# Two transformer blocks on one core: who squares for the norms, tiles read before weights are split, loop entries, and the order inside a recurrence

## The chip, the cores and the metric

One NeuronCore of a Trainium2 chip runs the whole program; everything else of the chip is idle. The metric is the device time of one execution in microseconds, taken as the median of several runs.

## The reference, cut to what matters

Two blocks in a row, 256 tokens of width 1024, all in float32. The first block has two layers and carries 256 context tokens along until its second layer; the second block has one layer with a gated recurrence and one with a pooling mixer.

```python
# first block, for each of 2 layers (512 tokens in layer 0; in layer 1 the context ends after the mixer's keys)
m = mixer(x * (1 + sc1) + sh1)         # Fourier mix, neighbourhood attention, latent attention, gated merge, @ w_out
x = layer_norm(ALPHA * x + (1 + g1) * m, ln1_g, ln1_b)
f = (silu(h @ w_gate) * (h @ w_up)) @ w_down          # h = x * (1 + sc2) + sh2, hidden width 2816
x = layer_norm(ALPHA * x + (1 + g2) * f, ln2_g, ln2_b)

# second block, layer 0 mixes by the recurrence, layer 1 by pooling
h = modulate(rms_norm(x, norm_mix_g), sh_m, sc_m)
gate = gelu(h @ w_y + b_y)
xr = causal_conv4(h @ w_in + b_in)
r, i = sigmoid(blockdiag(xr, w_a) + b_a), sigmoid(blockdiag(xr, w_x) + b_x)    # 4 blocks of 256 x 256 each
log_a = 8 * r * log_sigmoid(lam);  a = exp(log_a)
s = scan(a, sqrt(-expm1(2 * log_a)) * (i * xr))       # s_t = a_t * s_(t-1) + u_t along the tokens
y = (s * gate) @ w_out + b_out                        # layer 1: pool_mixer(h) * pool_scale
x = x + gt_m * y
x = x + gt_f * (square(relu(modulate(rms_norm(x, norm_ffn_g), sh_f, sc_f) @ w1)) @ w2)   # hidden width 4096
out = rms_norm(x, final_norm_g)
```

## The kernel before, in words

The residual stream stays in SBUF as `X`, eight tiles of 128 features by up to 512 tokens, and every product is built from two-part operands: a weight is `SH + SL`, an input `AH + AL` (or `HH + HL` for the hidden layer, `YH + YL` for branches and the convolved input), and each step takes three matmuls: high by high, high by low, low by high (L473, L474, L475).

The work is a hand-written list `seq` of sections. Most are a `Unit`: four output tiles, one PSUM bank each (banks 0 to 3), each over `kt` steps (8 mostly). Its weights come in two transfers of 1 MB (`RAW[0]`, `RAW[1]`, issued on SyncE, L425), each of which may start when the second split of the pair's old content is done. ScalarE copies a quarter of the weights to `SH` (`split_act`, L431), VectorE subtracts to get `SL` (`split_dve`, L437). There is one `SH` and one `SL` per tile position, so a unit's successor is split while the unit computes: as soon as the products of tile `m` are finished, ScalarE and VectorE split the successor's tile `m`, and then read tile `m` of their own unit out of its bank. A unit marked `by_k` does all four tiles' steps k by k (so that it can start while a norm still makes its inputs) and is finished with all four at once; one marked `late` leaves the last k-steps of its first two tiles to the end of those two.

What a unit does with a tile is in `read_act` and `read_dve`: `Residual` adds it to `X` on VectorE (L678), and behind it GpSimd keeps sums over features for the next norm (`stats_pool`, L646 to L657): per tile a total `S1`, a square `SQ` (L655) and the sum of squares `S2` (L657). `Norm` then sums over partitions with matmuls against ones into banks 4 and 5 (L808 to L814: `S1`, `S2`, the last tile of `X`, and its square `NT`, which ScalarE made at L885), makes mean and variance on VectorE (L829 to L839), the root on ScalarE (L889), the reciprocal on VectorE (L845), and then tile by tile centres, scales, casts to `AH` (L875) and subtracts to `AL` (L877). The norm of layer-norm kind that ends the first block is followed by a second, rms one.

Some units carry a side job: a 2 MB piece of the modulation weights `SIDE`, multiplied by the conditioning vectors on TensorE (L353), turned (L317) into banks 4 and 5 and added into `MODT` on VectorE (L375, `side.dve`).

Pairs of like units in the MLPs run in hardware loops of two turns. `write_programs` enters a loop (L2080) after TensorE has waited for the reader of every bank that the loop will use. There are four such entries where TensorE has to wait: the MLPs of both layers of both blocks.

The recurrence in order: a norm; two `Conv` units (`w_in`; per tile a bias copy to `XR` on ScalarE, L1636, the first tap on VectorE, L1646, three more, L1650, then `YH`, `YL`, L1653 and L1655); the first half of `w_y` (`Gelu`); four `GateBlocks` units of two k-steps (`w_a`, `w_x`, weights of 128x256 per split; sigmoid, L1677); `Lru` (tanh L1569, exp L1573, square L1577, sqrt L1580 on ScalarE, in two halves of four tiles; L1592, L1597 and the scan L1599 on VectorE); the second `Gelu`; `LruOut` (product with the gate on GpSimd, L1616, copy to `AH` on ScalarE, L1623, `AL` on VectorE, L1628); and `w_out`, two `Residual` units that add a bias first (L672, L675).

`PoolMix` multiplies by the pooling matrices `MIX` and `BT`, which `LoadWindows` brings from HBM after the first MLP of the second block (L1002), reads each of its tiles in two steps, and leaves the squares to GpSimd (L1754).

```python
        def act(self, e, K):                                    # Unit
            for m in range(4):
                e.wait_ge(sem["products"], K.at("products", self.freed(m)))
                if self.nxt:
                    self.nxt.split_act(e, K, m, 1 if self.loaded else 2)
                self.read_act(e, K, m)
```

## Time and profile before

| what | value |
|---|---|
| median of 3 runs | 2353.78 us |
| lowest and highest of them | 2350.56 and 2356.4 us |
| the profiled execution's own time | 2332.89 us |
| its span in the trace | 2331.1 us |
| mean granted TensorE clock in it | 0.947 of full |
| TensorE matmul busy | 2040.3 us |
| VectorE, ScalarE, GpSimd busy | 1216.7, 821.3, 192.4 us |

The rows come from one profiled execution, whose time is 20.9 us under the median of the other runs. Times in them are microseconds from the start of the span unless they say ns. `L473` is line 473 of the kernel. PE is TensorE's matmul side, PEld its weight loads, DVE is VectorE, ACT ScalarE, POOL GpSimd. In a timeline row the bracket at the end gives how long the engine had been idle before it and whose result ended that idle time. "PEclk" is the clock that TensorE was granted, as a share of 2.4 GHz.

### The profile page before, as it was taken

How to read it: one execution, taken by the hardware profiler on the slowest of the kernel's cores; microseconds unless marked ns; L12 is line 12 of the kernel's file. 1: busy time of each engine (PE TensorE's matmuls, PEld its weight loads, DVE VectorE, ACT ScalarE, POOL GpSimd, SP SyncE). 2: the span in 40 equal slices, each digit the busy share in tenths (PEclk: the TensorE clock that was granted, in tenths of full speed). 3: DMA queues.
4: the chain of work that ended last, by engine and by line, in shares of the span. 5: the costliest groups of instructions: out<-in, count | busy, mean ns of one | idle time of the engine just before them, and what ended most of it. 6: DMA issues, size and time to landing. Idle time of an engine off the chain costs nothing.

```text
span 2331.1 us, 31990 instructions
## 1 busy us (share of the span) xinstructions
PE 2040.3 (88%) x12456; PEld 1641.9 (70%) x12456; DVE 1216.7 (52%) x2075; ACT 821.3 (35%) x1314; POOL 192.4 (8%) x186
## 2 busy tenths in 40 slices
PE   3999899789979999998897979799968579986997
PEld 1777557247757777775774836689967579985997
DVE  6323544563564334345435564565666676666665
ACT  3422342262241121213424334343444633433343
POOL 0000000000300004012000000200330320011001
PEclk8999899899989999998999989899989789998999
DMA  7416025004534545545470704755532345642553
GB/s 271 146 60 218 30 73 167 0 2 162 170 129 156 195 145 192 169 155 169 138 250 1 239 1 159 258 180 168 193 109 73 115 138 164 191 152 91 175 186 109
DMA packets 280855, 332.07 MB, mean 142 GB/s; under 512 B 13286, under 2 KB 229788, under 8 KB 280604
## 3 DMA queue, kind: packets, MB, share of 16 engines
q1 hardware_dynamic: 268704, 323.05, 42.4%
q10 hardware_dynamic: 12028, 7.32, 1.2%
q8 instruction: 84, 1.38, 0.2%
q14 instruction: 39, 0.32, 0.0%
HBM read 329.31 MB, written 1.05 MB: 142 GB/s over the span
## 4 chain that ended last, share of the span: by engine, by line
PE 67%; issue 11%; DVE 9%; ACT 5%; DMA 5%; POOL 2%; ACTq 0%; POOLq 0%; DVEq 0%; SPq 0%
PE ps L473 17%; PE ps L474 16%; PE ps L475 16%; PE ps L1144 3%; DVE SL L437 3%; PE ps L353 3%; ACT SH L431 2%; PE ps L1166 2%; PE ps L1152 1%; DMA RAW<-in_w_in 1%; PE ps L1315 1%; DVE RSTD L845 1%; PE ps L1321 1%; DMA RAW<-in_ffn_w 1%; POOL S L657 1%
## 5 line engine op out<-in xcount | busy, mean ns | idle before, releaser
L437 DVE TENSOR_TENSOR SL<-RAW,SH 128x1024 fp32r<-128x1024 f32 (+3 forms) x460 | 529.2, 1154 | 836.0 <-ACT SH L431 834.7
L431 ACT ACTIVATE SH<-RAW 128x1024 fp32r<-128x1024 f32 (+3 forms) x460 | 447.6, 980 | 1110.2 <-PE ps L475 917.9
L473 PE MATMUL ps<-AH,SH 128*128 128x256 f32 (+1 forms) x2048 | 676.7, 330 | 84.8 <-DVE AL L877 28.5
L474 PE MATMUL ps<-AL,SH 128*128 128x256 f32 (+1 forms) x2048 | 668.1, 326 | 0.0
L475 PE MATMUL ps<-AH,SL 128*128 128x256 f32 (+1 forms) x2048 | 666.9, 326 | 0.0
L473 PEld LDWEIGHTS ps<-AH,SH 128*128 128x128 f32 x2048 | 401.3, 196 | 151.3 <-issue 53.3
L475 PEld LDWEIGHTS ps<-AH,SL 128*128 128x128 f32 x2048 | 400.9, 196 | 29.3
L474 PEld LDWEIGHTS ps<-AL,SH 128*128 128x128 f32 x2048 | 401.6, 196 | 27.4
L473 PE MATMUL ps<-HH,SH 128*128 128x256 f32 (+1 forms) x992 | 307.3, 310 | 8.8 <-DVE HL L747 4.5
L474 PE MATMUL ps<-HL,SH 128*128 128x256 f32 (+1 forms) x992 | 304.0, 306 | 0.0
L475 PE MATMUL ps<-HH,SL 128*128 128x256 f32 (+1 forms) x992 | 304.0, 306 | 0.0
L473 PEld LDWEIGHTS ps<-HH,SH 128*128 128x128 f32 x992 | 187.5, 189 | 29.7 <-issue 8.6
L475 PEld LDWEIGHTS ps<-HH,SL 128*128 128x128 f32 x992 | 187.1, 189 | 10.9
L474 PEld LDWEIGHTS ps<-HL,SH 128*128 128x128 f32 x992 | 187.1, 189 | 10.2
L649 POOL TENSOR_TENSOR S<-X 128x256 f32<-128x256 f32 (+1 forms) x9 | 13.1, 1451 | 1932.5 <-DVE X L678 1914.5
L353 PE MATMUL ps<-SIDE,CC 128*32 128x512 f32 x704 | 90.4, 634 | 14.6 <-DVE VAR L836 7.8
L473 PE MATMUL ps<-YH,SH 128*128 128x256 f32 (+1 forms) x224 | 75.7, 338 | 8.3 <-DVE YL L1071 3.0
L1200 ACT ACTIVATE PR<-ps,SM 128x512 f32<-128x512 f32 (+1 forms) x96 | 59.2, 616 | 65.8 <-PE ps L1152 52.6
L474 PE MATMUL ps<-YL,SH 128*128 128x256 f32 (+1 forms) x224 | 73.5, 328 | 0.0
L475 PE MATMUL ps<-YH,SL 128*128 128x256 f32 (+1 forms) x224 | 73.5, 328 | 0.0
L1240 DVE TENSOR_REDUCE SM<-ps 128x1 f32<-128x512 f32 (+1 forms) x96 | 57.4, 598 | 8.4 <-PE ps L1144 7.1
L1152 PEld LDWEIGHTS ps<-CON,PR 128*128 128x128 f32 x320 | 37.9, 147 | 31.5 <-issue 16.8
(240 smaller groups left out, 2032.9 us busy)
## 6 DMA issues: line engine op xcount, KB each, us to landing
SIDE<-in_w_mod SPq DMA_DIRECT2D x45, 2048.0 KB, 8.1
...
```

Of the source, the lines that this page charges most:

```text
L353: ins = e.matmul(PS[4][32 * g:32 * g + 32, :], CC[:, k, :], SIDE[:, k, :], start=k < 4, stop=k >= 4)
L431: e.activation(SH[:, m, 0:kt, :], RAW[p][:, 0:kt, o:o + P], ACT.Copy).then_inc(K.up("weight_high"), 1)
L437: e.tensor_tensor(SL[:, m, 0:kt, :], RAW[p][:, 0:kt, o:o + P], SH[:, m, 0:kt, :].bitcast(F32), ALU.subtract).then_inc(K.up("weight_low"), 1)
L473: e.matmul(ps, SH[:, m, k, :], xh, start=k == 0, stop=False)
L474: e.matmul(ps, SH[:, m, k, :], xl, start=False, stop=False)
L475: ins = e.matmul(ps, SL[:, m, k, :], xh, start=False, stop=k == self.kt - 1)
L657: e.tensor_tensor(S2[:, c0:c1], S2[:, c0:c1], SQ[:, c0:c1], ALU.add).then_inc(K.up("pool_done"), 1)
L1144: e.matmul(self.scores_of(n), q, k, start=True, stop=True).then_inc(K.up("scores_done"), 1)
L1152: ins = e.transpose(PS[self.TURNED[n % 2]][:, j * P:(j + 1) * P], PR[:, n % 2, j * P:(j + 1) * P], IDENT)
L1166: ins = e.matmul(o[64 * i:64 * i + 64, 0:256], V[:, c0 // P + j, 64 * (h + i):64 * (h + i) + 64], PTS[pair % 2][:, i, j, :], start=j == 0, ...
L1200: e.activation(PR[:, n % 2, 0:c1 - c0], self.scores_of(n), ACT.Exp, bias=SM[:, n % 4:n % 4 + 1], accum_out=SM[:, 4 + n % 4:5 + n % 4]).the ...
L1240: e.tensor_reduce(SM[:, n % 4:n % 4 + 1], ps, AX.X, ALU.max, negate=True).then_inc(K.up("max_done"), 1)
```

## The change

- **Tile first, weights second.** In every unit, ScalarE and VectorE read the finished tile out of its bank and only then split the successor's weights. VectorE also adds the side job (`side.dve`) before its last split.
- **Squares of the norms on ScalarE.** `Residual.read_act` squares the tile before the one just finished, into a ring of two buffers `SQR`; GpSimd only adds totals and squares. The norm's sums go to banks 6 and 7, which the side job does not use. In `PoolMix` ScalarE squares tiles in pairs, 512 wide, and the norm behind it sums both halves and the last pair with four matmuls.
- **Loop entries.** TensorE does not wait for a bank's reader in front of a loop where the loop's own first wait is on the same reader.
- **The recurrence.** The first tap of the convolution goes to ScalarE. The four `GateBlocks` units become one unit `Gates` with two transfers and four splits of 128x1024 over all eight banks. ScalarE does eight sigmoids, eight tanh, eight sigmoids, eight exp, eight sqrt and then the gelus, with the splits of the next units between them; the squares of the decay go to VectorE, 128x1024 at a time, and the scans run in two groups of four. `LruOut` is split in two and writes `Y8H`, `Y8L` with VectorE alone. The output bias is added into `X` by GpSimd ahead of time (`LruBias`), and the first `w_out` unit takes its inputs with four late k-steps in place of `by_k`.
- **The pooling matrices** get a place of their own and are loaded in front of the second block.

The diff, cut to its core:

```diff
+    MIX, BT = (MACC[:, 4 * j:4 * j + 4, :].rearrange("p g (t n) -> p g t n", t=2) for j in range(2))
...
@@ class Unit @@
         def act(self, e, K):
             for m in range(4):
                 e.wait_ge(sem["products"], K.at("products", self.freed(m)))
+                self.read_act(e, K, m)
                 if self.nxt:
                     self.nxt.split_act(e, K, m, 1 if self.loaded else 2)
-                self.read_act(e, K, m)
...
         def dve(self, e, K):
...
-                if self.nxt:
-                    self.nxt.split_dve(e, K, m)
                 e.wait_ge(sem["products"], K.at("products", m + 1))
                 self.read_dve(e, K, m)
                 if m == 3 and self.side:
                     self.side.dve(e, K, 0)
+                if self.nxt:
+                    self.nxt.split_dve(e, K, m)
...
+    class GeluLru(Gelu):
+        def act(self, e, K):
+            for k in range(KT):
+                e.activation(LA[:, k, :], LA[:, k, :], ACT.Exp, scale=DER[:, 6, k:k + 1]) \
+                    .then_inc(K.up("decay_done"), 1)
+            self.split_next(e, K, (0, 1))
+            for k in range(KT):
+                e.wait_ge(sem["one_minus_a2"], K.at("one_minus_a2", 4 * (k // 4) + 4))
+                e.activation(LT[:, k, :], LT[:, k, :], ACT.Sqrt).then_inc(K.up("root_done"), 1)
+            self.split_next(e, K, (2, 3))
+            for m in range(4):
+                self.read_act(e, K, m)
...
+        def dve(self, e, K):
+            for half in range(2):
+                t = slice(4 * half, 4 * half + 4)
+                e.wait_ge(sem["decay_done"], K.at("decay_done", 4 * half + 4))
+                e.tensor_tensor(XR[:, t, 0:SEQ], LA[:, t, :], LA[:, t, :], ALU.mult).then_inc(K.up("dve_done"), 1)
...
+            for m in (0, 1):
+                self.nxt.split_dve(e, K, m)
+            self.scan(e, K, 0)
+            for m in (2, 3):
+                self.nxt.split_dve(e, K, m)
+            self.scan(e, K, 1)
...
+    def stats_pool(e, K, first, tokens, mean):
...
+        def add_square(t):
+            e.wait_ge(sem["tile_squared"], K.at("tile_squared", t + 1 if first else t - 2))
+            if t > 1:
+                e.wait_ge(sem["square_added"], K.own("square_added"))
+            e.tensor_tensor(S2[:, c0:c1], S2[:, c0:c1], SQR[:, t % 2, c0:c1], ALU.add).then_inc(K.up("square_added"), 1)
...
     class Residual(Columns):
+        def read_act(self, e, K, m):
+            t = self.tile0 + m - 1
+            if not self.stats or t < 0:
+                return
+            c0, c1 = self.tokens
+            e.wait_ge(sem["dve_read"], K.at("dve_read", m))
...
+            to = S2[:, c0:c1] if t == 0 else SQR[:, t % 2, c0:c1]
+            e.activation(to, X[:, t, c0:c1], ACT.Square).then_inc(K.up("tile_squared"), 1)
...
@@ class Norm @@
-            for b in (4, 5):
+            for b in (6, 7):
                 reader, count = K.bank[b]
                 e.wait_ge(sem[reader], K.value(reader, count))
...
+            if self.paired:
+                e.matmul(PS[7][:, 0:n], ONES[:, :], S2[:, n:2 * n], start=False, stop=False)
+                e.wait_ge(sem["tile_squared"], K.at("tile_squared"))
+                e.matmul(PS[7][:, 0:n], ONES[:, :], SQR[:, 1, 0:n], start=False, stop=False)
+                ins = e.matmul(PS[7][:, 0:n], ONES[:, :], SQR[:, 1, n:2 * n], start=False, stop=True)
...
     class LoadWindows(Load):
         def act(self, e, K):
-            e.wait_ge(sem["dve_read"], K.at("dve_read"))
-            e.wait_ge(sem["products"], K.at("products"))
             e.wait_ge(sem["hidden_low"], K.at("hidden_low"))
...
+    class LruOut:
...
         def dve(self, e, K):
+            e.wait_ge(sem["products"], K.at("products", -self.products))
+            for j, k in enumerate(self.tiles):
+                e.wait_ge(sem["gated_done"], K.at("gated_done", j + 1))
+                e.tensor_copy(Y8H[:, k, :], XC[:, k, :]).then_inc(K.up("dve_done"), 1)
+                e.wait_ge(sem["dve_done"], K.own("dve_done"))
+                e.tensor_tensor(Y8L[:, k, :], XC[:, k, :], Y8H[:, k, :].bitcast(F32), ALU.subtract) \
...
+    class LruBias:
...
+            e.tensor_tensor(DER[:, 8, :], vec("lru_b_out_2", 0, 8), mod(2, 2, 2), ALU.mult).then_inc(K.up("pool_done"), 1)
+            e.wait_ge(sem["pool_done"], K.own("pool_done"))
             for k in range(KT):
+                e.tensor_scalar(X[:, k, 0:SEQ], X[:, k, 0:SEQ], DER[:, 8, k:k + 1], None, ALU.add) \
...
     class Conv(Copied):
         def read_act(self, e, K, m):
...
+            e.activation(XC[:, i, :], XR[:, i, 0:SEQ], ACT.Identity, bias=vec("lru_conv_b_2", i),
+                         scale=vec("lru_conv_w_2", i)).then_inc(K.up("tap_done"), 1)
...
-            e.tensor_scalar(xc, XR[:, i, 0:SEQ], vec("lru_conv_w_2", i), vec("lru_conv_b_2", i), ALU.mult, ALU.add) \
...
+    class Gates(Columns):
...
+        def act(self, e, K):
+            for p in range(2):
+                for i in range(KT):
+                    e.wait_ge(sem["products"], K.at("products", KT * p + i + 1))
+                    e.activation((GI if p else LA)[:, i, :], PS[i][:, 0:SEQ], ACT.Sigmoid,
+                                 bias=vec("lru_b_x_2" if p else "lru_b_a_2", i)).then_inc(K.up("act_read"), 1)
+                for m in range(2):
+                    self.nxt.split_act(e, K, 2 * p + m, 2)
+                if p == 0:
...
+                    for k in range(KT):
+                        e.activation(LT[:, k, :], LA[:, k, :], ACT.Tanh, scale=DER[:, 7, k:k + 1]) \
+                            .then_inc(K.up("act_done"), 1)
...
     class PoolMix(Residual):
+        def read_act(self, e, K, m):
+            to = S2[:, :] if m == 0 else SQR[:, m % 2, :]
+            e.wait_ge(sem["dve_read"], K.at("dve_read", m + 1))
...
+            e.activation(to.rearrange("p (j n) -> p j n", j=2), X[:, 2 * m:2 * m + 2, 0:SEQ], ACT.Square) \
...
+    seq.append(LoadWindows())
     seq.append(rms("norm_mix_g_2", 0, 2, 0, summed=True))
...
-    seq.append(gelu[0])
-    seq += [GateBlocks(w=A["lru_w_a_2"][0], u=u, dst=LA, bias="lru_b_a_2") for u in range(2)]
-    seq += [GateBlocks(w=A["lru_w_x_2"][0], u=u, dst=GI, bias="lru_b_x_2") for u in range(2)]
-    seq += [Lru(), gelu[1], LruOut()]
...
+    gelu[1].bank0 = 4
+    seq += [LruBias(), conv[0], conv[1], Gates(), gelu[0], LruOut(0, 4), gelu[1], LruOut(1, 8)]
...
-                     first=half == 0, mean=False, bias="lru_b_out_2", ready=("input_low", True), by_k=half == 0,
+                     first=half == 0, mean=False, folded=half == 0, rhs=(Y8H, Y8L), ready=("hidden_low", True),
+                     late=0 if half else 4, scale=lambda s, i: mod(2, 2, 2, i)) for half in range(2)]
...
-    seq.append(LoadWindows())
...
+    seq.append(rms("norm_ffn_g_2", 8, 3, 3, paired=True))
...
@@ write_programs @@
-                            eng.wait_ge(sems[before], count)
+                            if before != reader or v - stride[reader] < count:
+                                eng.wait_ge(sems[before], count)
```

TensorE at the third loop entry, where the first MLP of the second block passes from its first unit into the loop (`AH` is the norm's output, `HH` the hidden layer of the unit before). Before:

```order
L475 MATMUL ps<-HH,SL 128x256
L2080 UNCONDITIONAL_BRANCH [waits dve_read]
L2080 ISA
L466 REGISTER_ALU [waits weight_low]
L473 MATMUL ps<-AH,SH 128x256 [waits input_low,dve_read]
```

and with the change:

```order
L475 MATMUL ps<-HH,SL 128x256
L2152 UNCONDITIONAL_BRANCH
L2152 ISA
L466 REGISTER_ALU [waits weight_low]
L473 MATMUL ps<-AH,SH 128x256 [waits input_low,dve_read]
```

The wait at the branch is gone, and the one at the first matmul, which is counted per bank, stays.

ScalarE in the recurrence (`LA` the decay, `LT` what becomes the factor of the input, `GI` the input gate, `SH<-RAW` a split), before, from the first tanh on:

```order
L1569 ACTIVATE LT<-LA,DER 128x256 x4
L1573 ACT_TABLE_LOAD
L1573 ACTIVATE LA<-LA,DER 128x256 x4
L1577 ACTIVATE XR<-LA 128x256 x4
L1580 ACT_TABLE_LOAD
L1580 ACTIVATE LT<-LT 128x256 x4
L1569 ACT_TABLE_LOAD
L1569 ACTIVATE LT<-LA,DER 128x256 x4
L1573 ACTIVATE LA<-LA,DER 128x256 x4
L1577 ACTIVATE XR<-LA 128x256 x4
L1580 ACT_TABLE_LOAD
L1580 ACTIVATE LT<-LT 128x256 x4
```

and with the change, from the first sigmoid on:

```order
L1734 ACTIVATE LA<-ps,VEC 128x256 x8
L431 ACTIVATE SH<-RAW_54 128x1024 x2
L1742 ACTIVATE LT<-LA,DER 128x256 x8
L1734 ACTIVATE GI<-ps,VEC 128x256 x8
L431 ACTIVATE SH<-RAW_55 128x1024 x2
L593 ACT_TABLE_LOAD
L593 ACTIVATE LA<-LA,DER 128x256 x8
L431 ACTIVATE SH<-RAW_54 128x1024 x2
L598 ACT_TABLE_LOAD
L598 ACTIVATE LT<-LT 128x256 x8
L431 ACTIVATE SH<-RAW_55 128x1024 x2
```

The two rounds of tanh, exp and sqrt have become one, tanh has moved in front of the second eight sigmoids, and eight splits of 128x1024 stand between the steps.

ScalarE at the end of the recurrence's `w_out`, before:

```order
L431 ACTIVATE SH<-RAW_54 128x1024 x2
L431 ACTIVATE SH<-RAW_55 128x1024 x2
L885 ACTIVATE NT<-X 128x256
L887 ACT_TABLE_LOAD
L887 ACTIVATE SM<-ONES 128x1
```

and with the change:

```order
L761 ACTIVATE SQR<-X 128x256
L431 ACTIVATE SH<-RAW_54 128x1024
L761 ACTIVATE SQR<-X 128x256
L431 ACTIVATE SH<-RAW_54 128x1024
L761 ACTIVATE SQR<-X 128x256
L431 ACTIVATE SH<-RAW_55 128x1024
L761 ACTIVATE SQR<-X 128x256
L431 ACTIVATE SH<-RAW_55 128x1024
L958 ACTIVATE NT<-X 128x256
L960 ACT_TABLE_LOAD
L960 ACTIVATE SM<-ONES 128x1
```

A square of 128x256 now stands ahead of each split.

## Rows read from the trace of the kernel before

**Rows 1.** The page: busy time of each engine, and shares of the chain that ended last.
```profile
PE 2040.3 (88%) x12456; PEld 1641.9 (70%) x12456; DVE 1216.7 (52%) x2075; ACT 821.3 (35%) x1314; POOL 192.4 (8%) x186
...
PE 67%; issue 11%; DVE 9%; ACT 5%; DMA 5%; POOL 2%; ACTq 0%; POOLq 0%; DVEq 0%; SPq 0%
```

**Rows 2.** Windows: length; PE, PEld, DVE, ACT, POOL busy (count); PEclk, DMA share, GB/s.
```profile
777.00:790.00 13.00, 9.87 (x33) 7.97 (x34) 2.69 (x5) 1.86 (x3) 0.00 (x0) 0.74 0.68 225
1578.00:1582.00 4.00, 3.91 (x18) 3.94 (x19) 0.00 (x0) 0.00 (x0) 0.00 (x0) 0.50 1.04 339
1610.00:1630.00 20.00, 20.00 (x170) 20.00 (x170) 12.40 (x19) 7.90 (x10) 0.00 (x0) 1.00 0.52 175
1723.10:1727.00 3.90, 3.78 (x8) 2.50 (x8) 0.04 (x1) 0.00 (x0) 0.00 (x0) 0.50 0.04 13
1940.00:1953.00 13.00, 11.50 (x83) 11.53 (x84) 5.54 (x11) 3.77 (x6) 0.00 (x0) 0.87 0.31 90
```

**Rows 3.** Waits of TensorE: us in total, times, longest us.
```profile
PEld ps L473 <- DVE X L678: 14.8, 4, 4.1
PE ps L1144 <- DVE MODT L375: 13.2, 2, 6.6
```

**Rows 4.** Groups of instructions: count, busy us, mean ns, idle before and its releasers.
```profile
L437 DVE TENSOR_TENSOR SL<-RAW,SH 128x1024 fp32r<-128x1024 f32 x376 | 470.6, 1255 | 626.7 <-ACT SH L431 626.2
L431 ACT ACTIVATE SH<-RAW 128x1024 fp32r<-128x1024 f32 x376 | 394.8, 1058 | 866.4 <-PE ps L475 742.0 <-DMA RAW<-in_w_in 35.3 <-DMA RAW<-in_w_ffn_gate 29.0
L657 POOL TENSOR_TENSOR S<-S,SQ 128x256 f32<-128x256 f32 x36 | 34.0, 943 | 2.8
L678 DVE SCALAR_TENSOR_TENSOR X<-ps,DER,X 128x256 f32<-128x256 f32 x96 | 43.0, 475 | 0.0
L1650 DVE SCALAR_TENSOR_TENSOR XC<-XR,VEC,XC 128x256 f32<-128x256 f32 x24 | 11.6, 485 | 0.9
L1677 ACT ACTIVATE LA<-ps,VEC 128x256 f32<-128x256 f32 x8 | 3.7, 466 | 0.0
```

**Rows 5.** Timeline: the sums of the norm that ends the first block.
```profile
1723.14 1.22 PE L808 MATMUL ps<-S,ONES 128*128 128x256 f32 x2 [6.61 <-POOL S L657]
...
1726.96 0.42 DVE L829 TENSOR_SCALAR MU<-ps 128x256 f32<-128x256 f32 x1 [7.39 <-PE ps L814]
```

**Rows 6.** Timeline: where TensorE starts again at five other norms.
```profile
647.21 1.10 PE L808 MATMUL ps<-S,ONES 128*128 128x512 f32 x2 [3.18 <-DVE MODT L375]
...
1502.39 1.22 PE L808 MATMUL ps<-S,ONES 128*128 128x256 f32 x2 [4.64 <-POOL S L657]
...
1878.67 1.22 PE L809 MATMUL ps<-S,ONES 128*128 128x256 f32 x2 [5.98 <-POOL S L657]
...
2089.32 0.55 PE L1704 MATMUL ps<-SH,AH 128*128 128x256 f32 x1 [7.44 <-DMA MIX<-in_constants]
...
2115.27 1.22 PE L809 MATMUL ps<-S,ONES 128*128 128x256 f32 x2 [13.40 <-POOL S L1754]
```

**Rows 7.** Window of the recurrence, first split to last product of w_out; columns as rows 2.
```profile
1758.40:1872.70 114.30, 79.75 (x585) 75.95 (x583) 77.15 (x131) 63.20 (x118) 28.93 (x25) 0.90 0.35 111
```

**Rows 8.** Timeline inside the recurrence: last conv tile, ScalarE's steps, start of w_out.
```profile
1789.77 0.43 DVE L1655 TENSOR_TENSOR YL<-XC,YH 128x256 fp32r<-128x256 f32 x1
...
1816.74 1.71 ACT L1569 ACTIVATE LT<-LA,DER 128x256 f32<-128x256 f32 x4
...
1818.46 1.28 ACT L1573 ACT_TABLE_LOAD   x1
1819.76 1.71 ACT L1573 ACTIVATE LA<-LA,DER 128x256 f32<-128x256 f32 x4
...
1844.44 0.55 PE L473 MATMUL ps<-AH,SH 128*128 128x256 f32 x1 [16.65 <-DVE AL L1628]
```

**Rows 9.** The page: the products of the hidden layer, and what they wait for.
```profile
L473 PE MATMUL ps<-HH,SH 128*128 128x256 f32 (+1 forms) x992 | 307.3, 310 | 8.8 <-DVE HL L747 4.5
```

**Rows 10.** Timeline: where TensorE enters the Fourier mix.
```profile
110.06 2.18 PE L1031 MATMUL ps<-DFT,FT 128*128 128x256 f32 x9 [1.65 <-DVE MODT L375]
```

266 lines of the change are left out of this document (130 added, 136 removed).

## The prediction

> **What bounds the kernel now.** I read the page first. TensorE is busy with matmuls for 88% of the span and holds 67% of the chain that ended last; the next owner is "issue" with 11%, then VectorE with 9% [rows 1]. So the kernel is a stream of matmuls with holes, and an edit is worth what it takes out of the holes, plus what the clock does after them. Then the windows: in a steady stretch TensorE runs 170 matmuls in 20 us at granted clock 1.00, the level of 2.4 GHz, while after a hole it runs 18 in 4 us at 0.50, the level of 1.2 GHz, where the steady stretch would have run 34 [rows 2]. A hole thus costs its own length and a stretch at half speed behind it. Then the waits, for the holes with a name in the change: four at the loop entries, 14.8 us, and two in front of the neighbourhood attention, 13.2 us [rows 3]. The groups give durations [rows 4], and the timeline shows the holes at the norms [rows 5, 6] and in the recurrence [rows 7, 8].
>
> **Loop entries.** TensorE waits in front of the loop for a VectorE read that is queued behind the split of the last weights, 14.8 us over four entries [rows 3]. With the wait gone, the first matmul waits for its own bank only, which was read three tiles earlier; I leave 0.4 for each branch: 14.8 - 1.6 = 13.2 saved. The clock was 0.74 in the 13 us around one entry (of the two in the first block) and 0.87 around one of the second [rows 2]; if two entries are of each kind, the share lost is 13 x (0.26 + 0.26 + 0.13 + 0.13) = 10.1. I take 9, with 0 and 10.1 as ends. Sum 22.2.
>
> **Norm ends.** Before, GpSimd makes total, square and sum of squares for each tile, and TensorE has idled 6.61 us when the last sum comes [rows 5]. Afterwards ScalarE's square of tile 6 (0.45 us, the length of a 256-wide read [rows 4]) starts when the last product ends, and GpSimd's addition (0.94 [rows 4]) follows: TensorE starts at about 1.4. The last square comes after one split of 1.06 [rows 4], at about 2.0, behind the first matmuls. That is 5.2 saved; the eight sum matmuls behind took 3.78 us at clock 0.50 [rows 2], and after a short hole part of that comes back, 0.8. In all:
> - end of the first block: 5.2 + 0.8 = 6.0
> - first norm of layer 1: 4.64 [rows 6] less 1.4, and 1.2 from the clock: 4.4
> - norm behind the recurrence: 5.98 [rows 6] less 1.4, and 0.5: 5.1
> - the two norms over 512 tokens: TensorE waits 3.18 there for the side job's addition [rows 6]. With other banks that wait is not needed, but squares of 512 (0.63) and an addition of 1.3 (both estimates, twice the elements of the rows for 256, less the fixed part) bring about 2.0: 1.2 each, 2.4
> - norm behind PoolMix: 13.40 us of hole [rows 6], of which GpSimd's seven squares are the end. Afterwards VectorE and ScalarE take turns tile by tile: a read in two steps 0.9, a square of 512 0.63, a split 1.06, a split 1.25 [rows 4]: 3.8 us for each of four tiles, so the wait falls by 3.1
> - norm before PoolMix 0.5; the final norm loses 0.8, since ScalarE's square stands between VectorE's last read and the addition.
>
> Together 2.4 + 4.4 + 6.0 + 5.1 + 3.1 + 0.5 - 0.8 = 20.7.
>
> **Pooling matrices.** TensorE waited 7.44 us for them [rows 6]. Loaded far ahead, the wait ends with the norm's second `AL` at 5.8: 1.6 saved.
>
> **Recurrence.** Before, 114.3 us pass from the first split behind the first `Conv` to the last product of `w_out`, with TensorE busy for 79.75 [rows 7]. The new order, laid out with the old durations from 1758.4 on:
> - VectorE per conv tile: three taps of 0.485 [rows 4], cast and subtract 0.7, split 1.25 [rows 4]: 3.4, where it was 3.8. But the second `Conv`'s first weights wait for the whole first tile: 2.2 later. Eight tiles end at 1785.5 to 1787; before, the last `YL` was at 1789.8 [rows 8].
> - ScalarE then is the chain: eight sigmoids 3.7 [rows 4], two splits 2.1, eight tanh 3.4 (four were 1.71 [rows 8]), eight sigmoids 3.7, two splits 2.1, a table load 1.3 [rows 8], eight exp 3.4, two splits 2.1, a table load 1.3, eight sqrt 2.7, two splits 2.1, a table load 1.3, four gelus 1.9: 31.1 us from 1787, to about 1815 to 1818. Two table loads are gone, 2.6 us.
> - VectorE behind it: eight scans with splits between, the second half of `w_y` on TensorE, and the last `Y8L` at about 1830 to 1831. Before, `w_out` started at 1844.44 after 16.65 us of hole [rows 8]. The first k-steps of `w_out` start earlier, its last 16 + 32 + 32 steps of three matmuls at 0.12 us follow: end at about 1850.9.
> So the stretch falls from 114.3 to 92.5: **21.7** saved. I bound this from both sides by 5 (ScalarE's chain with every split waiting for a late transfer) and 30 (all of the hole of 16.65 [rows 8] gone, and three quarters of the other 17.9 in which TensorE stands, 114.3 - 79.75 - 16.65).
>
> What a table load costs is seen in the trace: it takes 1.28 us, starts 10 ns after the last tanh ended, and the exp starts 20 ns behind it [rows 8]. The Trainium skill, "ScalarE: Activation LUTs", section "What ACT_TABLE_LOAD costs", gives about 1.28 us for the load and about 1.38 for a drain beside it. By that, two loads fewer would be worth 5.3 us rather than 2.6, and my stretch would be 2.7 shorter; the trace agrees with the first part and shows no second one.
>
> **Small places.** Side additions come one split earlier at VectorE: the Fourier mix waits 0.35 rather than 1.65 [rows 10], twice, 2.6; the attention's two waits [rows 3] shorten by 1.0 each, 2.0. The hidden layer's low half is ready a split earlier, so its waits of 4.5 [rows 9] go, with 0.6 of bank waits: 5.1. Against this, splits come later by a read in all units: a `by_k` unit whose four tiles end together gives its successor its first weights 0.4 to 1.2 us later, 3.4 in sum, and the values 1.2. Net 2.6 + 2.0 + 5.1 - 3.4 - 1.2 = 5.1. The delayed split costs nothing elsewhere, because the units' weights are split a whole unit ahead; its cover is the idle time of VectorE, 52% busy [rows 1]. If the cover is gone, a unit waits for `SL`, which is the last rival.
>
> **Sum.** 22.2 + 20.7 + 1.6 + 21.7 + 5.1 = 71.3. The rows are of an execution of 2332.9 us, which comes to 2261.6; that execution is 20.9 under the median of the runs, and I subtract the same from the median: 2353.8 - 71.3 = **2283**.
>
> **Rivals.**
> - *Half of the norm and recurrence gains, 15%.* ScalarE becomes the bound where it has splits, squares and table loads in one queue. For: in the recurrence it is busy 63 of 114 us already [rows 7]. Against: the norms' square is 0.45 beside 1.06. It loses (20.7 + 21.7)/2 = 21: 2304.
> - *The clock falls in new places, 8%.* The side job's rows run early, holes move, and the clock term of 9 fails with as much again lost at other stretches like those of 1.2 GHz [rows 2]: 2300.
> - *The clock term is nothing, 5%.* If what the rows call a granted clock did not slow the matmuls, shorter holes would give back their length only: 9 less, 2292. Against it: 18 matmuls in 4 us at 0.50, 170 in 20 at 1.00 [rows 2]. The Trainium skill, "TensorE: Matmul & The Clock Gate", section "Seeing it yourself", warns that clock events in a trace have been seen to be unreliable; by that this term could be 0. The trace disagrees, since the spacing of the matmuls changes with the clock shown.
> - *The loop entry does nothing, 2%.* The matmul behind the branch waits for the same read, so the change does not do what it says there: 22 less, 2305.
> - *Slower, 4%.* Reading first makes each split later by a read (0.47 for a 256-wide one on ScalarE, 0.475 on VectorE [rows 4], 1.1 for a gated or squared one). The buffer `RAW` comes free later by both, its transfer lands later, and in the 256-token stages (36 units in layer 1, 42 in the second block), where a unit lasts some 11.6 us (96 matmuls of 0.12) and needs 2 MB, TensorE waits for `SL` at each unit. This cancels everything from 71.3/78 = 0.9 us per unit on. At 1.2 us it costs 94: 2376. Against it: in the steady stretch DMA is at 0.52 and TensorE never idle [rows 2], so there is slack of several us per unit.
>
> **Numbers.** The forecast has 66%, the rivals the rest. Predicted 2283. Its own ends: recurrence +17 / -8, clock +9 / -1, small places and norms some 8 either way. With the first two rivals inside, the range is 2266 to 2312, which leaves out about 2 in 10. A measurement of this kernel can tell about 0.3%, some 7 us, from no change. Faster by more than that: all cases but the last, and a rest of 1%: 0.95; slower 0.04; same 0.01.
>
> **What would show it.** In the profile after: no wait of the first products at the four loop entries for L678's successor, and a clock of 1.00 in the 13 us behind; TensorE's hole in front of the norm's sums at 1.5 to 2 rather than 4.6 to 6.6; no wait for the pooling matrices; 27 table loads on ScalarE in place of 30; and the recurrence at 92 us in place of 114. The prediction is wrong if the splits' waits of TensorE ("PEld L473 <- DVE SL") grow by tens of us in the stages of 256 tokens, if a hole of over 4 us stands at the loop entries with another releaser, or if the recurrence's stretch stays over 105.

## The result, and the profile after

The changed kernel takes 2253.3 us (median of 4 runs, 2250.97 to 2256.18) where the kernel before takes 2353.7: a ratio of 0.9574, with a 95% interval of 0.9557 to 0.9592. That is 100 us less, where 71 were forecast, and it lies below the range, whose low end was 2266. The direction was right and the size was not.

Between the two profiled executions, the sum that was forecast, the spans differ by 81.9 us (2331.1 to 2249.2). The other 18.5 us are in how quick the two profiled executions were: the one before lay 20.8 us under its median, the one of the changed kernel 2.3 under its own. The first experiment below explains it.

Part 1 of the page of the changed kernel:

```profile
PE 2021.5 (90%) x12460; PEld 1630.8 (73%) x12460; DVE 1221.5 (54%) x2045; ACT 842.7 (37%) x1357; POOL 139.3 (6%) x121
```

Span less PE's busy time is the time in which TensorE stands: 290.8 before [rows 1], 227.7 now, 63.1 less. The matmuls themselves, of about the same number, take 18.8 less. So the gain has two kinds, holes and clock, and they are kept apart below.

The windows of the changed kernel, with the columns of [rows 2]: two loop entries in the first block (TensorE enters the loops at 777.4 and 1551.8), one in the second (1873.1), a steady stretch, and the sums of the norm that ends the first block.

```profile
776.00:789.00 13.00, 13.00 (x64) 10.40 (x63) 4.05 (x7) 2.72 (x3) 0.00 (x0) 1.00 0.97 322
1546.00:1559.00 13.00, 13.00 (x114) 13.00 (x114) 7.66 (x10) 5.06 (x6) 0.00 (x0) 1.00 0.79 248
1872.00:1885.00 13.00, 13.00 (x112) 13.00 (x112) 8.71 (x15) 5.85 (x8) 0.00 (x0) 1.00 0.60 184
1576.00:1596.00 20.00, 20.00 (x169) 20.00 (x169) 11.85 (x17) 8.50 (x11) 0.00 (x0) 1.00 0.63 206
1691.00:1693.10 2.10, 1.99 (x8) 1.44 (x8) 1.38 (x4) 1.95 (x4) 0.01 (x1) 1.00 0.35 123
```

The clock at the entries is 1.00 where it was 0.74 and 0.87 [rows 2], and the eight sum matmuls take 1.99 us where they took 3.78. The waits at the entries, 14.8 us over four [rows 3], are gone. In the waits of the changed kernel below, the first line is the wait of weight loads for split weights, which the prediction's slower rival had growing by tens of us; it was 56.0 before. The second is the wait in front of the two neighbourhood attentions, 13.2 before. The third has the engine and releaser of the old waits at the entries, but stands elsewhere: four waits of 0.8 us of the weight loads inside the down products of the first block's layer 0 (at 896, 921, 1043 and 1068 us), for which the matmuls do not stop.

```profile
PEld ps L473 <- DVE SL L437: 28.8, 18, 6.6
...
PE ps L1215 <- DVE MODT L374: 11.1, 2, 5.5
...
PEld ps L473 <- DVE X L732: 3.4, 4, 0.8
```

The timeline of the changed kernel at the norms of [rows 5, 6] (in this order: first norm of layer 1, end of the first block, behind the recurrence, pooling product, behind PoolMix):

```profile
1485.28 0.70 PE L876 MATMUL ps<-S,ONES 128*128 128x256 f32 x2 [0.39 <-POOL S L711]
...
1691.07 0.70 PE L876 MATMUL ps<-S,ONES 128*128 128x256 f32 x2 [1.46 <-POOL S L711]
...
1817.85 0.70 PE L877 MATMUL ps<-S,ONES 128*128 128x256 f32 x2 [1.31 <-POOL S L711]
...
2017.92 0.55 PE L1774 MATMUL ps<-SH,AH 128*128 128x256 f32 x1 [5.80 <-DVE AL L950]
...
2039.29 1.22 PE L877 MATMUL ps<-S,ONES 128*128 128x256 f32 x2 [7.58 <-POOL S L1828]
```

The holes of 4.64, 6.61 and 5.98 are 0.39, 1.46 and 1.31, and TensorE starts on the pooling matrices after 5.80 us, which is the wait for the norm, all as forecast; the one behind PoolMix fell by 5.8 rather than 3.1.

The window of the recurrence, first read behind the first `Conv` to the last product of `w_out`, and a table load in it:

```profile
1724.50:1816.60 92.10, 76.10 (x586) 74.66 (x584) 73.10 (x105) 60.09 (x102) 21.23 (x21) 0.93 0.45 143
```
```profile
1770.00 1.28 ACT L598 ACT_TABLE_LOAD   x1
1771.29 0.42 ACT L598 ACTIVATE LT<-LT 128x256 f32<-128x256 f32 x1
```

92.1 us, where 92.5 were laid out and 114.3 stood before [rows 7].

### The profile page after: what moved, and what is told of

It reads as the page before. It is cut to its first block and busy times, and to the rows that moved or that the text cites. A ratio compares the mean times of both kernels' runs of the same rounds, so it can differ in the third digit from the quotient of the medians.

```text
span 2249.2 us, 31789 instructions
## 1 busy us (share of the span) xinstructions
PE 2021.5 (90%) x12460; PEld 1630.8 (73%) x12460; DVE 1221.5 (54%) x2045; ACT 842.7 (37%) x1357; POOL 139.3 (6%) x121
## 3 DMA queue, kind: packets, MB, share of 16 engines
q8 instruction: 84, 1.38, 0.3%
## 5 line engine op out<-in xcount | busy, mean ns | idle before, releaser
L437 DVE TENSOR_TENSOR SL<-RAW,SH 128x1024 fp32r<-128x1024 f32 (+2 forms) x448 | 525.2, 1176 | 482.8 <-ACT SH L431 477.1
L473 PE MATMUL ps<-AH,SH 128*128 128x256 f32 (+1 forms) x1984 | 652.9, 329 | 57.7 <-DVE AL L950 39.4
L474 PE MATMUL ps<-AL,SH 128*128 128x256 f32 (+1 forms) x1984 | 645.7, 325 | 0.0
L475 PE MATMUL ps<-AH,SL 128*128 128x256 f32 (+1 forms) x1984 | 644.6, 325 | 0.0
L431 ACT ACTIVATE SH<-RAW 128x1024 fp32r<-128x1024 f32 (+2 forms) x448 | 443.4, 997 | 457.3 <-PE ps L475 309.4
L473 PEld LDWEIGHTS ps<-AH,SH 128*128 128x128 f32 x1984 | 384.5, 194 | 119.3 <-issue 65.8
L475 PEld LDWEIGHTS ps<-AH,SL 128*128 128x128 f32 x1984 | 384.3, 194 | 29.2
L474 PEld LDWEIGHTS ps<-AL,SH 128*128 128x128 f32 x1984 | 384.6, 194 | 27.4
L473 PE MATMUL ps<-HH,SH 128*128 128x256 f32 (+1 forms) x992 | 305.3, 308 | 2.7 <-DVE HL L691 1.6
L473 PEld LDWEIGHTS ps<-HH,SH 128*128 128x128 f32 x992 | 186.3, 188 | 22.4 <-issue 4.2
L475 PEld LDWEIGHTS ps<-HH,SL 128*128 128x128 f32 x992 | 186.4, 188 | 10.9
L705 POOL TENSOR_TENSOR S<-X 128x512 f32<-128x512 f32 (+1 forms) x6 | 10.9, 1816 | 1524.2 <-DVE X L732 1524.2
L732 DVE SCALAR_TENSOR_TENSOR X<-ps,DER,X 128x256 f32<-128x256 f32 x96 | 43.2, 478 | 94.0 <-PE ps L475 94.0
L473 PE MATMUL ps<-YH,SH 128*128 128x256 f32 (+1 forms) x256 | 85.1, 332 | 9.5 <-DVE SL L437 6.4
L711 POOL TENSOR_TENSOR S<-S,SQR 128x256 f32<-128x256 f32 (+1 forms) x54 | 50.9, 942 | 472.3 <-ACT SQR L761 472.3
```

The lines of the kernel that those rows point to most:

```text
L431: e.activation(SH[:, m, 0:kt, :], RAW[p][:, 0:kt, o:o + P], ACT.Copy).then_inc(K.up("weight_high"), 1)
L437: e.tensor_tensor(SL[:, m, 0:kt, :], RAW[p][:, 0:kt, o:o + P], SH[:, m, 0:kt, :].bitcast(F32), ALU.subtract).then_inc(K.up("weight_low"), 1)
L473: e.matmul(ps, SH[:, m, k, :], xh, start=k == 0, stop=False)
L474: e.matmul(ps, SH[:, m, k, :], xl, start=False, stop=False)
L475: ins = e.matmul(ps, SL[:, m, k, :], xh, start=False, stop=k == self.kt - 1)
L705: e.tensor_tensor(S1[:, c0:c1], so_far, X[:, t, c0:c1], ALU.add).then_inc(K.up("pool_done"), 1)
```

## The experiments

Times are medians of 5 to 12 runs beside runs of the kernel before on the same chip; its medians there were 2348.3, 2348.9, 2347.7 and 2351.7. "us saved" is against that median. The 95% intervals of their ratios come to 6 to 8 us either way. "Hole time" is the span of the profiled execution less the time in which TensorE's matmuls are busy.

### The kernel before, again

No edit. Expected:

> The kernel before, unchanged, with a profile taken on this chip. What is to be told: its profiled execution was 2332.9 us while its runs have a median of 2353.7; the change saved 81.9 us between the two spans and 100.4 between the medians. Theory A (the trace of before was an unusually quick execution; the missing 18.6 us sit at places that have nothing to do with the change): the new profiled execution takes 2350 to 2356, and the 20 us lie in stretches like the first block's attention. Theory B (profiling itself makes this kernel quicker, by its timing at the loop entries or at the clock): the new one is again at 2330 to 2336 while the runs stay at 2353.

Measured: 2351.1, from 2346.5 to 2361.6; 19 other runs of it on this chip lay between 2334.1 and 2357.8. Its new profiled execution has a span of 2352.7. Part 1 of its page, and windows of the two neighbourhood attentions, first in it, then in the execution shown ahead of the prediction:

```profile
PE 2061.7 (88%) x12456; PEld 1654.3 (70%) x12456; DVE 1217.8 (52%) x2075; ACT 821.5 (35%) x1314; POOL 192.3 (8%) x186
```
```profile
266.00:354.00 88.00, 80.64 (x368) 47.58 (x364) 45.35 (x124) 39.83 (x111) 0.00 (x0) 0.86 0.15 49
1256.00:1314.00 58.00, 52.87 (x272) 31.66 (x272) 30.53 (x72) 24.95 (x60) 0.00 (x0) 0.78 0.17 56
```
```profile
265.00:347.00 82.00, 74.63 (x366) 44.31 (x363) 45.35 (x124) 39.61 (x111) 0.00 (x0) 0.93 0.16 52
1245.00:1296.00 51.00, 45.28 (x272) 27.84 (x268) 30.32 (x72) 24.78 (x59) 0.00 (x0) 0.92 0.19 63
```

TensorE stands for 291.0 us in one and 290.8 in the other: the same. All of the 21.6 us between them is matmul time at a lower granted clock, and 11.6 of it lies in these two stretches (5.5 and 6.1 between the first matmuls of each attention and of what follows it; the windows are rounded to whole us). Theory A holds, though only about half of the difference lies in the attentions. Over the 31 runs of this batch the time broadly follows the mean granted clock: 0.946 goes with 2334 us, 0.933 with 2357. The profile ahead of the prediction, at 0.947, was one of the quickest executions that this kernel has.

### The loop entries alone, and undone

```diff
-                            eng.wait_ge(sems[before], count)
+                            if before != reader or v - stride[reader] < count:
+                                eng.wait_ge(sems[before], count)
```

Expected, for this edit on the kernel before:

> The kernel before with the loop-entry edit alone. By the forecast it saves 22.2 us (13.2 of waits, 9 of clock): about 2331. Rival (clock term is nothing): 13 us, 2340. Rival (the wait only moves): 0 to 2 us.

Measured: 2326.1 (ratio 0.990, 0.987 to 0.994), 22.2 us saved, as forecast; the interval is 14 to 31 us. In its profile all four waits at the entries are gone, and the hole time is 280.9 us, 10.1 less than in the repeated kernel before, where 13.2 were forecast. The rest of the 22 is matmul time.

The same lines put back in the changed kernel. Expected:

> The changed kernel with the old wait at the loop entries. If the parts add up, it loses the same 22 us: about 2275. If tiles read first already let the last read come sooner, the wait is shorter by one split of 1.25 us at each of four entries, and it loses 12 to 18: 2266 to 2271.

Measured: 2259.1, 5.8 more than the 2253.3 of the changed kernel, and 8.5 more than its second median below. It is less than either expectation. Its waits have `PEld ps L473 <- DVE X L732: 10.9, 8, 2.4`: four of these eight are at the entries, 7.6 us with the longest 2.4, where the kernel before has 14.8 and 4.1; the other four are the 0.8 us ones that the changed kernel has too. The entries are worth 22 us alone and 6 to 8 beside the rest.

### The order of reading and splitting, undone and alone

In the changed kernel:

```diff
                 e.wait_ge(sem["products"], K.at("products", self.freed(m)))
-                self.read_act(e, K, m)
                 if self.nxt:
                     self.nxt.split_act(e, K, m, 1 if self.loaded else 2)
+                self.read_act(e, K, m)
...
+                if self.nxt:
+                    self.nxt.split_dve(e, K, m)
                 e.wait_ge(sem["products"], K.at("products", m + 1))
                 self.read_dve(e, K, m)
                 if m == 3 and self.side:
                     self.side.dve(e, K, 0)
-                if self.nxt:
-                    self.nxt.split_dve(e, K, m)
```

Expected:

> The changed kernel with the weights split first and the tiles read second, in every unit that keeps the common order. By the forecast the order brings 9.7 us in small places and costs 4.6, and behind it stand parts of the norm terms, since the square would wait for a split of 1.06 us: loses 5 to 15, 2258 to 2268. Rival (reading first is what delays splits and transfers): it gains, 2240 to 2250. If the unexplained 18.6 us belong to this part, it loses 25 or more.

Measured: 2291.6, 38 to 41 us more than the changed kernel, and 21 to 23 us more hole time (249.1). The expected 5 to 15 was too little.

The same order put into the kernel before, alone. Expected:

> The kernel before with tiles read first and weights split second, and nothing else. Undone in the changed kernel this order was worth 38 us. If the order alone brings that, by the loop entries (the last read is no longer queued behind a split), by the units that need all four banks, and by the norms' sums, it takes 2308 to 2318. If it needs the squares on ScalarE to bring it, 2330 to 2340. If it steadies the clock in the neighbourhood attention (0.86 and 0.74 in the repeated execution of before, 0.88 and 0.93 in the changed kernel), its runs lie within 6 us of each other.

Measured: 2288.2 (ratio 0.975, 0.972 to 0.978), from 2283.4 to 2294.6: 60.7 us saved by this one edit, over half of the whole, and 20 us beyond the quickest that was expected. The clock in the attentions is not steadied by it, since later runs fall on either side. The page of this run:

```profile
PE 2022.1 (88%) x12456; PEld 1632.7 (71%) x12456; DVE 1246.8 (55%) x2075; ACT 823.7 (36%) x1314; POOL 209.9 (9%) x186
```

Against the repeated kernel before, TensorE stands 27 us less (291.0 to 264.0 of a span of 2286.1) and its matmuls take 39.6 less; some 15 of these are the two attentions, which came out quick in this execution. Of the 27, 6 are at the loop entries (14.9 us of waits in the repeated kernel before, 8.7 here) and about 10 in front of the norms' sums, places that the forecast had given to other edits. The wait of weight loads for split weights is 54.8 us here and 58.0 there, so the later split delayed nothing. How a shorter hole gives back more than itself is seen at one loop entry of the first block, here 17 us around it in the repeated kernel before and in this run:

```profile
784.00:801.00 17.00, 13.27 (x56) 10.55 (x55) 3.32 (x5) 2.60 (x3) 0.00 (x0) 0.80 0.59 200
```
```profile
769.00:786.00 17.00, 15.49 (x76) 12.52 (x75) 4.63 (x6) 4.15 (x5) 0.00 (x0) 1.00 0.61 208
```

The wait of TensorE in it (put down to the side job's addition) fell from 3.73 to 1.50 us, and the granted clock behind it is 1.00 instead of 0.80: 76 matmuls in 17 us instead of 56. In this stage (the norm of layer 0 to the next one) the hole time fell by 3.0 us and the length by 10.7:

```profile
653.90:1087.40 433.50, 418.13 (x2000) 311.00 (x2001) 179.30 (x266) 100.05 (x120) 46.94 (x38) 0.97 0.49 163
```
```profile
643.30:1066.10 422.80, 410.38 (x2000) 307.54 (x2001) 188.99 (x263) 100.10 (x120) 56.27 (x38) 0.99 0.49 167
```

### The order on one engine at a time

The changed kernel with the first half of the edit above (ScalarE splits first), and with the second (VectorE; `PoolMix` keeps the changed order there). Expected:

> The changed kernel with ScalarE splitting first and reading second, VectorE as changed. Of the 38 us of the order, ScalarE's part is the tiles that ScalarE reads (gates, silu, squared relu) and the norm squares, each of which would wait for a split of 1.06 us. If the order matters on the way of a tile to the next unit's input, both engines' parts count and this one loses 10 to 20 (2262 to 2272). If it is VectorE alone (reads of the residual, side additions), it loses under 5.

Measured: 2269.8, 19 more than the changed kernel (2250.6).

> The changed kernel with VectorE splitting first and reading second (in PoolMix it stays as changed), ScalarE as changed. VectorE's split is 1.25 us and first waits for ScalarE's, which now comes after ScalarE's read: a read on VectorE is late by up to 2.3 us. If the bank and the loop entries wait for VectorE's read, this is the larger half: loses 20 to 40 (2272 to 2292). If under 10, the order's worth lies on ScalarE.

Measured: 2293.8, 43 more: as much as both halves together, and a little over the 20 to 40 expected. The hole time is 236.8 and 250.7 in these two, against 226.5 to 227.7 in the changed kernel. So VectorE's order carries it; ScalarE's 19 vanish when VectorE already splits first. The reason given for the 43 is argued from the waits, not isolated: VectorE's reads end the waits at entries, at the side additions and at units that need all four banks. In this run the two attentions wait 13.3 us for `MODT` and four norms up to 6.1 us for GpSimd, against 11.1 and at most 2.0.

### Both edits on the kernel before

> The kernel before with tiles read first and with the loop-entry edit. Alone they saved 60.7 and 22.2 us. If they remove different waits they add up: 2266. If the wait at the entries was mostly the read queued behind the split, reading first has already taken it, and the pair is worth what the entry edit was in the changed kernel, 5.8, more than the order alone: 2280 to 2284.

Measured: 2281.7 (0.969 to 0.974 of before), 66.1 us saved, against 60.7 for the order alone; 60.7 and 22.2 would be 82.9. The two edits meet at the entries: the read that TensorE awaited there was queued behind the split, and the order alone takes 6 of the 15 us of waits. Yet it is not the hole time that fails to add up. It is 252.4 here, 38.6 less than in the repeated kernel before, and 27.0 and 10.1 for the two alone make 37.1; why the 6 us are not missing was not traced. What does not add up is the clock behind the holes. In the 13 us around the entries (3 before TensorE goes on, 10 after) it was 0.74, 0.74, 0.74 and 0.87 in the repeated kernel before, and the order alone had brought three of the four to 1.00, so the second edit had little left to give back. The second entry in these two, first in the repeated kernel before, then with the order alone:

```profile
1593.50:1606.50 13.00, 10.00 (x62) 10.03 (x63) 4.06 (x6) 2.88 (x5) 0.00 (x0) 0.74 0.51 163
```
```profile
1547.60:1560.60 13.00, 10.87 (x91) 10.71 (x91) 6.79 (x10) 5.71 (x7) 0.00 (x0) 1.00 0.52 164
```

### Squares back on GpSimd

A first form put the squares on GpSimd but kept the new division of tiles between units, with tile 3 in the second one. Expected:

> The changed kernel with the squares of the layer norms and of the MLP norms back on GpSimd (PoolMix keeps its pairs). By the forecast's norm terms it loses what GpSimd's chain costs at five norms, 2.4 + 4.4 + 6.0 + 5.1 + 0.5 less the part that the other banks give: 10 to 18, so 2263 to 2271. Rival: GpSimd starts earlier than before because tiles are read a split sooner, so the square's place is worth only 5 to 8: 2258 to 2261.

Measured: 2316.0, 65 more. That was the edit and not the part: tile 3's square waited for the last read of the second unit, since it counted reads from that unit's start, and the waits of TensorE show GpSimd's chain behind it at `PEld ps L874 <- POOL S L714: 48.5, 4, 15.1`. The second form takes `stats_pool` of the kernel before:

```diff
-                stats_pool(e, K, self.first, self.tokens, self.mean)
+                c0, c1 = self.tokens
+                stats_pool(e, K, self.first, range(self.tile0, min(self.tile0 + 4, KT - 1)), c0, c1, self.mean,
+                           "dve_read")
...
         def read_act(self, e, K, m):
-            t = self.tile0 + m - 1
...
-            e.activation(to, X[:, t, c0:c1], ACT.Square).then_inc(K.up("tile_squared"), 1)
+            return
```

Expected:

> The changed kernel with the statistics of its residual units made on GpSimd word for word as before (each unit its own tiles, no square on ScalarE; PoolMix keeps its pairs). The first form of this run had made the square of tile 3 wait for the last read of the second unit, which put GpSimd's whole chain of up to 15 us behind the products. Forecast's norm terms: loses 10 to 18, 2261 to 2269. Rival, from the run with tiles read first alone (it is 8.5 us ahead of the changed kernel when layer 1 reaches the neighbourhood attention, and behind by 11 at the norm that ends the first block): over 512 tokens GpSimd keeps up and ScalarE's square costs, over 256 tokens the square saves; the two nearly cancel, 2248 to 2258.

Measured: 2249.9 (5 runs, 2248.3 to 2258.1), the same as the changed kernel. Windows from the norm of layer 0 to the next, and from the norm of layer 1 to the one that ends the block, first in the changed kernel, then in this run:

```profile
651.10:1075.80 424.70, 412.63 (x2001) 308.42 (x2001) 182.00 (x264) 107.32 (x134) 42.46 (x24) 0.98 0.50 166
1485.30:1691.10 205.80, 197.54 (x1665) 191.55 (x1665) 135.50 (x207) 93.02 (x127) 21.41 (x24) 0.99 0.62 199
```
```profile
644.40:1065.30 420.90, 410.88 (x2009) 307.86 (x2004) 189.16 (x264) 100.17 (x120) 56.27 (x38) 0.99 0.50 168
1483.40:1695.50 212.10, 199.14 (x1665) 192.64 (x1665) 136.86 (x208) 88.53 (x112) 39.67 (x38) 0.97 0.60 194
```

Over 512 tokens GpSimd's squares are 3.8 us quicker in this stage; over 256 tokens ScalarE's are 6.3 us quicker. The second profile of the changed kernel has the same two lengths within 0.1 us. The holes in front of the sums say why. In this run:

```profile
644.44 1.13 PE L859 MATMUL ps<-S,ONES 128*128 128x512 f32 x2
...
1483.42 0.80 PE L859 MATMUL ps<-S,ONES 128*128 128x256 f32 x1 [2.00 <-POOL S L708]
...
1695.45 0.80 PE L859 MATMUL ps<-S,ONES 128*128 128x256 f32 x1 [5.92 <-POOL S L708]
```

and in the changed kernel, over 512 tokens (the two others, 0.39 and 1.46, stand above):

```profile
651.06 1.13 PE L876 MATMUL ps<-S,ONES 128*128 128x512 f32 x2 [1.89 <-POOL S L711]
...
1075.80 2.07 PE L876 MATMUL ps<-S,ONES 128*128 128x512 f32 x2 [2.04 <-POOL S L711]
```

The norms behind residual units of the second block also start earlier with GpSimd's squares: behind the recurrence after 0.13 us instead of 1.31, and before `PoolMix` and at the end with no hole instead of 1.31. In the whole they cancel: the hole time is 226.8 here.

### Sums in banks 4 and 5

```diff
-            for b in (6, 7):
+            for b in (4, 5):
...
-                e.matmul(PS[6][:, 0:n], ONES[:, :], S1[:, c0:c1], start=True, stop=whole)
-            ins = e.matmul(PS[7][:, 0:n], ONES[:, :], S2[:, c0:c1], start=True, stop=whole)
+                e.matmul(PS[4][:, 0:n], ONES[:, :], S1[:, c0:c1], start=True, stop=whole)
+            ins = e.matmul(PS[5][:, 0:n], ONES[:, :], S2[:, c0:c1], start=True, stop=whole)
```

> The changed kernel with the norm's sums in banks 4 and 5 as before. Forecast: only the two norms over 512 tokens and the first norm of layer 1 wait for the side job's addition: loses 1 to 4, 2254 to 2257. Rival: since the addition now comes a split earlier, nothing is lost: 2251 to 2254.

Measured: 2246.9 (2245.6 to 2252.6), 3.7 less than the changed kernel in the same batch. Both expectations missed: moving the sums to banks 6 and 7 does not help here and may cost. The holes in front of the sums over 512 tokens are 1.88 and 2.04 us in this run, as in the changed kernel, so there the sums wait for the squares and not for the side job. The intervals of the two ratios overlap, and what makes it is left open.

### The changed kernel again

> The changed kernel again, for a second profile and more runs. The kernel before takes 2334 to 2358 over its runs, a spread of 1%, and two profiled executions of it differ by 20 us, of which 12 lie in the two neighbourhood attentions, at granted clocks of 0.95 and 0.92 against 0.86 and 0.74. Theory C (the change makes those stretches steady): all runs within 2250 to 2257 and the same clocks of about 0.88 and 0.93. Theory D (it is chance, and four runs were too few to show it): a run of 2262 or more turns up.

Measured: 2250.6, from 2244.6 to 2260.4. Theory C fails: the runs spread over 16 us. The sign of theory D, a run of 2262 or more, did not come either, but its content is seen: the profiled execution, with a span of 2258.6, has the second attention at a clock of 0.77, near the 0.78 of the repeated kernel before, and the first at 0.89. The first line is of the first profile of the changed kernel, the second of this one:

```profile
1240.00:1292.00 52.00, 46.06 (x269) 28.30 (x270) 30.80 (x73) 24.88 (x59) 0.00 (x0) 0.91 0.20 65
1241.00:1298.00 57.00, 51.95 (x266) 30.75 (x263) 30.63 (x72) 24.88 (x59) 0.00 (x0) 0.77 0.18 58
```

### What is left when order, squares, banks and entries are undone

The edits above together, in the changed kernel: recurrence, early pooling matrices and PoolMix's pairs stay.

> The changed kernel with four parts undone together: weights split first, statistics on GpSimd as before, sums in banks 4 and 5, the wait at the loop entries. What is left of the change is the recurrence, the early pooling matrices and PoolMix's squares in pairs. From the stretches of the traces: recurrence and the norm behind it 26 to 27, pooling matrices 1.6, PoolMix 3: 31 less than before, 2316 to 2320. With the pair of order and entry (66 alone) that closes the sum of about 97. If the parts lean on one another (the new recurrence needs tiles read first), it saves under 22: over 2326.

Measured: 2329.1 (ratio 0.991, 0.989 to 0.994), 22.6 saved where 31 were expected. Windows from the second norm between the blocks to the norm behind the recurrence, in the kernel before, in this run and in the changed kernel:

```profile
1732.70:1878.70 146.00, 100.07 (x689) 92.73 (x689) 97.40 (x176) 76.70 (x145) 34.53 (x29) 0.87 0.30 95
```
```profile
1744.20:1865.90 121.70, 98.27 (x688) 91.84 (x689) 90.81 (x146) 70.85 (x121) 36.89 (x38) 0.89 0.38 122
```
```profile
1698.80:1817.80 119.00, 96.40 (x688) 91.42 (x688) 88.60 (x144) 72.80 (x127) 29.58 (x31) 0.89 0.38 123
```

The stretch brings its 24 us alone and 27 with the rest. Over the whole kernel, spans and TensorE's busy time are of the profiled executions, and the time saved is between medians:

| run | span | matmuls busy | hole time | hole time less | time saved |
|---|---|---|---|---|---|
| kernel before, again | 2352.7 | 2061.7 | 291.0 | | |
| entries alone | 2317.3 | 2036.4 | 280.9 | 10.1 | 22.2 |
| order alone | 2286.1 | 2022.1 | 264.0 | 27.0 | 60.7 |
| order and entries | 2277.4 | 2025.0 | 252.4 | 38.6 | 66.1 |
| the rest alone | 2319.0 | 2056.2 | 262.8 | 28.2 | 22.6 |
| changed kernel, again | 2258.6 | 2032.1 | 226.5 | 64.5 | 98.3 |

The holes add up: 38.6 and 28.2 make 66.8, where the whole change has 64.5. The time does so less well, 88.7 of 98.3, but each of these three numbers has an interval of 6 to 7 us either way, so that it is not shown that the parts bring more together than alone. The time that the matmuls give back on top of the holes is shown to come with the order (60.7 against 27.0); the rest alone shows none (22.6 against 28.2).

### A version from the runs

The changed kernel with sums in banks 4 and 5, and GpSimd's statistics as before only where a unit has 512 tokens.

```diff
-                stats_pool(e, K, self.first, self.tokens, self.mean)
+                c0, c1 = self.tokens
+                if c1 - c0 > SEQ:
+                    stats_wide(e, K, self.first, range(self.tile0, min(self.tile0 + 4, KT - 1)), c0, c1, self.mean,
+                               "dve_read")
+                else:
+                    stats_pool(e, K, self.first, self.tokens, self.mean)
```

> A version built from the runs: the changed kernel with the norm's sums in banks 4 and 5, and with the statistics made on GpSimd alone where a unit has 512 tokens (first block, layer 0), on ScalarE and GpSimd where it has 256. Banks 4 and 5 gave 3.7 (2246.9 against 2250.6). GpSimd over 512 tokens was 8 to 10 us ahead of the changed kernel where layer 1 begins, of which 2 to 3 are also in the run with banks 4 and 5. If the two add up: 2239 to 2242. If the gain over 512 tokens was the clock of one execution: 2246 to 2248.

Measured: 2244.1 (2238.6 to 2248.8), ratio 0.9546 (0.9519 to 0.9572), between the two expectations: the lowest of all, though its interval overlaps that of the changed kernel (0.9557 to 0.9592) and the two were not run side by side, so a gain over it is not shown. Its stages, as above:

```profile
646.20:1068.60 422.40, 412.53 (x2001) 308.40 (x2001) 188.98 (x264) 100.12 (x120) 56.24 (x38) 0.98 0.50 167
1485.00:1690.10 205.10, 198.26 (x1664) 190.51 (x1664) 135.73 (x207) 92.62 (x126) 21.13 (x24) 0.98 0.61 197
```

Each stage is within 1.5 us of the better of the two above. In this version TensorE waits 0.95 us for the side job's addition (`MODT`) in front of the sums over 512 tokens, where the run with GpSimd's squares and banks 6 and 7 has no hole: with these squares banks 6 and 7 are the better place. No run has them together with ScalarE's squares over 256 tokens.

## Why the prediction was right in its direction and wrong in its size

The step that failed is the clock term. The sum counted 11.5 us of quicker matmuls, 9 at the loop entries and 2.5 at the norms' sums, and none behind the holes that reading first would shorten. By the medians it was about 37 us: 100.4 saved, of which 63.1 is hole time. With the order alone it was 34 (60.7 less 27.0). The rows could show only part of it, since they came from a quick execution. The 29.1 us between 71.3 and 100.4 are 3.3 of holes, 7.3 of clock that even the quick execution shows (18.8 for 11.5), and 18.5 from the subtraction from the median. The range could not hold it either: it allowed the clock 1 us more than was counted.

- **The holes as a sum: right.** Of the 71.3, about 60 were hole time (71.3 less 9 of clock at the entries and 2.5 at the sums). Measured between the spans: 63.1, and 64.5 between the two repeated executions. But which edit brings them was not as laid out, as the next points say.
- **"I subtract the same from the median": wrong, 18.5 us.** The text took the 20.9 us between profiled execution and median as an offset that both kernels share. It is granted clock that the execution happened to have. The changed kernel's first profiled execution was also the quickest of its four, but only 2.3 under their median; its second one was 10 over its median. The difference of the medians is a better measure than that of two single executions.
- **The clock: mis-sized.** 11.5 were counted, at the entries and the sums only. Against the quick execution the matmuls are 18.8 us shorter, against the repeated one 40.2. Of the 40.2, some 10 lie in the two attentions, where two executions of one kernel differ as much by chance. Holes that the order shortens have a stretch behind them, as the loop entry shown above has, and the text priced those holes by their length.
- **"Small places", net 5.1: the edit priced too low.** Its items came as laid out: the attentions wait 5.55 each for 6.6, the Fourier mix 0.7 for both entries instead of 3.3. But reading first alone saves 60.7, with 27.0 of hole time. The text counted 4.6 for the splits' delay, of which the waits for split weights show nothing, and left the reads that had stood behind a split of 1.25 us in the terms of others: it put them under the entries (22.2, alone right, beside the order 6 to 8) and under the squares.
- **Norm ends, 20.7: the places right, the reason wrong in part.** The holes over 256 tokens fell to 0.4 to 1.5 as laid out, and the two over 512 tokens from 3.18 to 1.89 and 2.04, which is the forecast 1.2 each. But with GpSimd's squares back the total is the same. The squares on ScalarE save 1.6 and 4.5 us at the two norms over 256 tokens of the first block and cost 1.2 to 2.0 at five others. Over 512 tokens it is the order that shortened the holes (3.18 to 0.96 with the order alone), and the squares gave some of it back. The norm before `PoolMix` lost 0.6 (0.69 to 1.31) where 0.5 was to be gained.
- **Recurrence: right.** 92.1 us for 92.5. ScalarE's chain was laid out instruction by instruction, and the last `YL` ended at 1797.15, which is 1831.0 on the old axis, where 1830 to 1831 stood. The agreement to 0.4 us is partly luck: ScalarE was through the fifth gelu at 1779.0, 1812.9 on the old axis and so 2 to 5 us ahead of the text, and VectorE behind it took as much longer.
- **Pooling matrices: right** at 5.80. **PoolMix:** 5.8 saved for 3.1; with the weights split first in the changed kernel its hole is 10.65, so that about half of the 5.8 hangs on the order.
- **Table loads.** There are 27 for 30, as forecast. The load shown above for the changed kernel takes 1.28 us and its sqrt starts 10 ns behind it. The extra 1.38 us of the Trainium skill ("ScalarE: Activation LUTs", "What ACT_TABLE_LOAD costs") shows here no more than before; the measurement decides, 2.6 us for two loads and not the 5.3 estimated from the page's figures.
- **The rival from "TensorE: Matmul & The Clock Gate"** of the Trainium skill, that clock events in a trace may be unreliable and the clock term nothing: refuted. Two executions of the kernel before with the same hole time (290.8 and 291.0) differ by 21.6 us, as their granted clocks do, and over 31 runs the time goes with the clock. The run with the entries alone saved 22, with a lower end of 14, where its holes give 10.
- **The slower rival:** its premise fails. DMA is at 0.63 in the steady stretch and TensorE without a hole; the wait of weight loads for `SL`, its sign, was to grow by tens of us and went from 58.0 to 54.8 with the order alone; in the changed kernel, with the new recurrence, it is 28.8.
